# First expert's down product moved ahead of the turning of the second block's rows, its weights third in the stream

## What is computed

```
def expert_block(args):
    xblk, e = args
    h = jax.nn.silu(xblk @ w_gate[e]) * (xblk @ w_up[e])
    return h @ w_down[e]
```

## Time and profile before

| what | us |
|---|---|
| median of 3 runs | 3432.39 |
| lowest and highest of them | 3426.86, 3435.41 |
| the profiled execution | 3430.01 |
| its span in the profile | 3428.5 |

### The profile page before, as it was taken

One profiled execution on the slowest core, in us unless ns is written; L12 is line 12 of the kernel. 1 busy time (PEld: TensorE's weight loads), 2 busy tenths in 40 slices (PEclk: granted clock), 3 DMA queues, 4 the chain that ended last, 5 costly groups with the idle time before them and its releaser, 6 DMA issues. The chain is left out here.

```text
span 3428.5 us, 39709 instructions
## 1 busy us (share of the span) xinstructions
PE 3266.1 (95%) x15466; PEld 2344.9 (68%) x15466; DVE 1497.5 (44%) x2662; ACT 812.2 (24%) x1791; POOL 859.9 (25%) x537
## 2 busy tenths in 40 slices
PE   8999999989999999999999999989899999899998
PEld 7857767765444786776666544458677766788886
DVE  5575502331111656556644111152687522455552
ACT  3363311021111345432322111121222121211100
POOL 5214122310000430320003100023354231253352
PEclk9999999999999999999999999999899999999999
DMA  3251121148887331122232788861101122112221
GB/s 153 110 229 50 74 98 74 50 177 299 324 324 291 121 120 50 42 91 108 92 129 98 282 324 324 320 243 70 50 29 54 53 96 98 50 74 85 88 98 50
DMA packets 50270, 470.77 MB, mean 137 GB/s; under 512 B 5792, under 2 KB 6176, under 8 KB 26400
## 3 DMA queue, kind: packets, MB, share of 16 engines
q1 hardware_dynamic: 27072, 379.00, 29.9%
q0 software_dynamic: 21136, 78.39, 5.8%
q10 hardware_dynamic: 1872, 10.75, 0.8%
HBM read 506.65 MB, written 63.18 MB: 166 GB/s over the span
## 5 line engine op out<-in xcount | busy, mean ns | idle before, releaser
L638 PE MATMUL bank<-B,ring 128*128 128x256 f32 x4336 | 953.5, 380 | 24.4 <-ACT B L770 9.2
L638 PEld LDWEIGHTS bank<-B,ring 128*128 128x128 f32 x4336 | 824.8, 191 | 146.8 <-issue 33.7
L622 POOL TENSOR_TENSOR ring<-ring 128x1024 f32<-128x1024 f32 x58 | 149.7, 2580 | 1178.6 <-DMA ring<-in_w_static 378.7
L2057 PE MATMUL bank<-ring,B 128*128 128x512 f32 x960 | 419.1, 594 | 0.3 <-issue 0.2
L770 ACT ACTIVATE B<-bank 128x256 f32<-128x256 f32 x356 | 135.1, 384 | 971.2 <-PE bank L638 945.7
L2057 PEld LDWEIGHTS bank<-ring,B 128*128 128x128 f32 x960 | 180.2, 190 | 218.8 <-issue 218.8
L638 PE MATMUL bank<-XT,ring 128*128 128x256 f32 x1344 | 305.6, 381 | 22.8 <-DMA ring<-in_w_static 15.3
L541 PE MATMUL bank<-B,ring 128*128 128x512 f32 x704 | 305.2, 592 | 1.0 <-ACT B L2842 1.0
L638 PEld LDWEIGHTS bank<-XT,ring 128*128 128x128 f32 x1344 | 256.3, 191 | 63.6 <-issue 29.2
L541 PEld LDWEIGHTS bank<-B,ring 128*128 128x128 f32 x704 | 133.7, 190 | 161.9 <-issue 159.8
L2132 DVE TENSOR_TENSOR B<-B,bank 128x512 f32<-128x512 f32 x46 | 31.6, 688 | 462.2 <-PE bank L2057 406.3
(11 more groups left out here) (501 smaller groups left out, 4051.8 us busy)
## 6 DMA issues: line engine op xcount, KB each, us to landing
ring<-in_w_expert SPq DMA_DIRECT2D x96, 2048.0 KB, 9.1
ring<-in_w_static SPq DMA_DIRECT2D x79, 2048.0 KB, 8.4
B<-in_w_expert SPq DMA_DIRECT2D x42, 2048.0 KB
slots_y<-B POOLq DMA_DIRECT2D x52, 512.0 KB
B<-slots_x POOLq DMA_DIRECT2D x44, 512.0 KB
slots_x<-B POOLq DMA_DIRECT2D x23, 512.0 KB
ring<-s_tables SPq DMA_DIRECT2D x4, 2048.0 KB, 8.5
s_tables<-tmp POOLq DMA_DIRECT2D x8, 512.0 KB, 3.8
```

Source lines behind the costliest of these rows:

```text
L622: pool.tensor_tensor(s(0), w(1, 0), w(1, 1), ALU.add).then_inc(made.up(), 1)
L638: ins = pe.matmul(out, left, right, start=start and k == 0, stop=k == 3, skip_group_check=not start)
L2057: ins = pe.matmul(bank[:, :], xbT[q % 2][:, k, :], slot[:, k, :], start=k == 0, stop=k == KT - 1)
```

## The change

The down product of block 0 goes to the front of the `experts` stage. TensorE's list now begins `turn_hidden(0)`, `down(0)`, `turn_rows(1)`, `gate_and_up(1)`, `turn_rows(2)`, `turn_hidden(1)`, `gate_and_up(2)`, `turn_rows(3)`, `down(1)`, and goes on as before. The `hold_clock` in `turn_rows(1)` is gone. ACT copies the hidden values of block 0 right after the silu of block 0 and before the rows of block 1; DVE copies out the down result of block 0 before it multiplies the hidden values of block 1. In the stream the down weights of block 0 stand third: gate 0, up 0, down 0, gate 1, up 1, gate 16, up 16, down 1.

```
@@ expert_chunks
-        if q:
+        if q == 0:
+            names.append(("down", l, n))
+        if q > 1:
             names.append(("down", l, BLOCK_ORDER[q - 1]))
@@ turn_rows
-                if q == 1:
-                    hold_clock(m, pe, bk.bank(("xbT", l, q, 0)), 7)
@@ tensor
-            for q in range(nb - 1):
-                if q >= 1:
+            turn_hidden(0)
+            down(0)
+            turn_rows(1)
+            for q in range(1, nb - 1):
+                if q > 1:
                     turn_hidden(q - 1)
-                    gate_and_up(q)
+                gate_and_up(q)
                 if q + 2 < nb:
                     turn_rows(q + 1)
-                if q >= 1:
+                if q > 1:
                     down(q - 1)
@@ scalar
             for q in range(nb + 1):
-                if q >= 1:
-                    o = q - 1
...
+                if q > 1:
+                    keep_hidden(q - 1)
                 if q < nb:
...
+                if q == 0:
+                    keep_hidden(0)
                 if q + 1 < nb:
                     keep_rows(q + 1)
@@ vector
             hidden(0)
+            keep_rows(0)
             for q in range(1, nb - 1):
                 hidden(q)
-                keep_rows(q - 1)
+                if q > 1:
+                    keep_rows(q - 1)
```

More of the change, by code:

```diff
@@ L2108, in keep_rows, with keep_hidden @@
                                             bank[:, :].rearrange("p (a b) -> p a b", a=4), ACT.Copy).then_inc(bk.free_sem(("xbT", l, q, i)), 1)
+            def keep_hidden(o):
+                act.wait_ge(*bk.made(("hT", l, o)))
+                bank = bk.bank(("hT", l, o))
+                act.activation(hidT[o % 2], bank[:, :].rearrange("p (a b) -> p a b", a=4), ACT.Copy).then_inc(bk.free_sem(("hT", l, o)), 1)
             for q in range(nb + 1):
-                if q >= 1:
-                    o = q - 1
-                    act.wait_ge(*bk.made(("hT", l, o)))
-                    bank = bk.bank(("hT", l, o))
-                    act.activation(hidT[o % 2], bank[:, :].rearrange("p (a b) -> p a b", a=4), ACT.Copy).then_inc(bk.free_sem(("hT", l, o)), 1)
+                if q > 1:
+                    keep_hidden(q - 1)
                 if q < nb:
```

## The result

The changed kernel took **3446.98 us** (median, 3440.63 to 3455.59), the kernel before 3434.52 us beside it: ratio **1.0038**, 95% interval 1.0027 to 1.0049, that is 12.5 us or 0.38% slower. A second measurement gave 3445.23 against 3433.95, ratio 1.0034 (1.0025 to 1.0044). The forecast was 3440.9 us, a ratio of 1.0025. The time lies in the range of 3434 to 3448, but on the other side of the 0.3% that I had drawn as the border of "no change".

What follows compares the result with a forecast made beforehand. TensorE's own list was taken to bound the stage; per layer 0.27 + 0.73 + 2.2 - 0.88 + 0.73 + 1.3 = 4.35 us, 8.5 us over both layers, gave 3440.9 us on the median, range 3434 to 3448.

Steps and rivals of the forecast that it cites:

- The chain from the barrier: Steps from the barrier to the start of block 1's down product: 4.3 us later in the first layer, 4.2 second.
- The handoff to the down product: Before block 0's down product: TensorE waits 0.73 us for ACT's copy of the hidden values just turned.
- that to gate and up: Before block 1's gate and up: 0.73 us of new idle time, waiting for ACT's two copies of the rows.
- B: Stretch from ACT's table load behind the barrier to block 1's down product; the stretch the forecast was made for.
- The low clock: Block 0's down product runs partly at half speed after the idle time: 2.2 us lost per layer, bounds 1.4 to 3.15.
- the clock returns late: Rival at block 0's down product: 3.15 instead of 2.2 us lost per layer, time 3442.8; chance 0.36, shared with handoff's upper bound.
- My rule of 4.4 us: Full clock returns 4.4 us after block 0's down product starts; half the work until then is lost, 2.2 us.
- Edits costed at nothing: Weight stream order, POOL's row loads, DVE's and ACT's copies: no cost; the stream's slack stays or grows.
- in the profile the old list has no wait for data at its start: Start of the experts stage before the change: only the barrier and the hold stand there; block 1's rows are present.
- A: Stretch from block 0's first gate matmul to ACT's table load behind the barrier; not in the forecast at all.
- Rows arrive late: Rival at the wait for block 1's rows: they land late in ordinary executions, the down product fills that wait; 3422, chance 0.04.
- same: Outcome within about 0.3%, or 10.3 us, of no change; chance 0.60, from the forecast's 0.52 and paced elsewhere 0.08.

Runs made afterwards that it cites:

- the second profile: The changed kernel measured and profiled again, nothing altered: 3445.23 us against 3433.95 for the kernel before, ratio 1.0034.
- after: The changed kernel as described, against the kernel before: 3446.98 us, ratio 1.0038.
- the late load: Fifth weight load issued only once block 1's rows have landed: old order 3418.51 us; changed order with throw-away products put back 3430.15 us.
- the stream alone: The kernel before with its engine lists and hold, taking only the new order of weight loads: 3435.76 us against 3432.43, ratio 1.0006.

## Why the prediction was right or wrong

**The chain from the barrier was right, step by step.** The hidden transposes were forecast 2.66 us after the start of ACT's table load and came after 2.67. The handoff to the down product took 0.73 us, that to gate and up 0.79 for 0.73. From gate and up to block 1's down product it was 17.12 us (787.88 to 805.00) for 17.02. B was forecast as 32.2 and measured as 31.83 and 32.6, and 32.06 and 32.8 in the second profile.

**The low clock was sized about right.** The down product lost 1.4, 2.2, 1.7 and 2.4 us in the four layers profiled, for a forecast of 2.2 and bounds of 1.4 to 3.15; the four transposes took 1.12 us for 0.85. The rival "the clock returns late" asked for 3.1 us or more and did not happen. My rule of 4.4 us after the product's start held in the second layer (4.4 us) and not in the first (2.9 us). On transposes the prediction read too much out of the earlier trace rows: the clock did return while transposes ran, but 2.4 us of throw-away products stood ahead of them. The kernel before without its hold is the better row: behind a stretch of 3.35 us, transposes with one short wait, the clock was back 0.9 us after the first product, sooner than in either layer of after.

**Edits costed at nothing** held in the changed kernel: no weight load stood as releaser before its products. That the slack of the stream can only stay or grow was too strong: with the old lists the new stream made TensorE wait 0.67 and 1.07 us, too little for the medians (1.0006). Leaving out the hold in the old order changed nothing that the medians can tell (1.0001). In the changed order the medians put the hold at 6 to 8 us (1.0016 against 1.0034 and 1.0038), more than the low clock of one product, by which the prediction priced its removal; with touching intervals, and a profile that does not have this gain, its worth there is not settled.

**What failed is the sentence "in the profile the old list has no wait for data at its start".** It holds for the list, but I took the barrier as given at 773.0 and did not ask what opened it. It is opened by POOL's read of block 1's rows, and the trace I read had caught an A of 17.3 us where the kernel ordinarily has about 20. So the sign of error that I had named last, the old kernel's wait for rows in other executions, did show, but not where the rival "Rows arrive late" put it: the wait stands at the barrier, ahead of the down product, which can't fill it. This did not change the difference between the kernels, since A is about 20 in both, but it hid where time is to be had: TensorE is idle for 6 us there in the old order as well, and holding one load back gains 15 us.

**What stays open.** B accounts for some 8.6 us; 12.5 and 11.3 were measured. Between the second profiles of the two kernels (spans 3442.5 and 3432.3) 7.1 us lie in A and B together, 2.1 from there to the second layer's A, 0.9 behind its B, 0.2 ahead of the first A. With the late load the same holds: 7.3 us in A and B, 11.6 in the medians. All thirteen profiles together say more. The span without A and B is 3336.2 to 3344.9 us in the six with the new lists (mean 3339.4) and 3330.6 to 3338.0 in the seven with the old lists (mean 3334.9). So some 4 us go with the new lists, though the two ranges overlap. They do not lie in the rest of the experts stages: from block 1's down product to the end of the last one it is 328.1 us in the first layer and 327.7 in the second, in every profile but that of the stream alone. They lie where both kernels run the same code: from the first layer's last down product to the second layer's A (768.0 against 766.5 us in the mean) and from the second layer's last down product to the end (1161.8 against 1158.2). Why the new lists should lengthen these stretches no run shows.

**The number and the chances.** The chances of 0.60 for "same" and 0.36 for "slower" came from a sum of 8.5 us, just inside a border at 10.3 us; with 3 us outside the stage it fell just beyond. The sign was right, and so were the place and the size of the 8 us in the stage. That the time stayed inside the range is partly luck: it lies 1 us below the upper end, and what carried it there, some 3 us outside the stage and a median of before 2.1 us higher (3434.52 for 3432.39), is no term of the sum. (The lower end should be 3432.1 by its own sum, 3437.6 - 5.5, and not 3434.)

## What to carry to other kernels

Two steps that hand a result to each other through another engine need a third step between them on the engine that bounds the kernel; moving a product forward took that cover away in three places at 0.5 to 0.8 us each and filled no wait. Where all engines meet at a barrier, ask first which engine's last DMA opens it: here one weight load, needed only 19 us behind the barrier, delayed the rows and with them a small read on which every engine waited. A single profile can sit several microseconds off a kernel's usual pattern, so profile the kernel before twice before pricing an edit of 4 us.

## What was not expected of the hardware

POOL waited 9.3 to 10.2 us behind its last scatter for the rows to land when a 2 MB load started 2.1 to 2.2 us after the start of that scatter, and 4.1 to 4.9 us when the load was held back. The one exception is the first trace, where the load started 2.5 us after it: 5.5 us in both layers. With an idle time of 1.09 us at the barrier and a hold behind it, TensorE's clock stayed at 2.4 GHz; without the hold, in a wait of 1.42 us after 1.06 us of transposes, it fell to 1.2 GHz in one layer and stayed up in the other.
